# Router logits as four partial rows, tokens 0 to 127 last in a normalisation, and a token scatter issued in two pieces, in a two-layer hybrid decoder step

## What is computed

```python
x = layer_norm(ALPHA * x + mix, P['ln_mix_g'][l], P['ln_mix_b'][l])
...
logits = (jnp.einsum('btd,de->bte', x, router) + router_b).astype(jnp.float32)
probs = jax.nn.softmax(logits, axis=-1)
top_p, top_i = lax.top_k(probs, TOP_K)
...
for e in range(N_EXPERTS):
    y = y + gates[..., e:e + 1] * swiglu(x, w1[e], w3[e], w2[e]).astype(jnp.float32)
```

## Time and profile before

| what | value |
|---|---|
| three timed runs | 1055.07, 1058.78 and 1060.44 us, median 1058.78 us |
| the profiled execution | 1055.58 us, of it a span of 1053.8 us |
| granted TensorE clock, mean | 0.989 of full speed |
| PE busy | 1029.1 us, 98% of the span, 10347 records |
| DVE, ACT, POOL busy | 433.7, 182.0 and 94.2 us |
| memory traffic | 240.17 MB, mean 228 GB/s |

### The profile page before, as it was taken

The page is one execution under the profiler, slowest core; times in us unless marked ns, Lnnn a source line. Parts: engine busy times, 40 slices in busy tenths (PEclk is TensorE's granted clock), DMA queues, the critical chain, the costliest instruction groups (busy, mean ns, idle before and its releaser), DMA issues.

```text
span 1053.8 us, 22738 instructions
## 1 busy us (share of the span) xinstructions
PE 1029.1 (98%) x10347; PEld 736.3 (70%) x10347; DVE 433.7 (41%) x852; ACT 182.0 (17%) x393; POOL 94.2 (9%) x102
## 2 busy tenths in 40 slices
PE   9999999999999999999999999997999999999995
PEld 6787766999999999987877669743444444444452
DVE  5654635565656754256546352512011011010125
ACT  1322224031111100133322240500000000000011
POOL 2010123700000000000101200041000020000020
PEclk9999999999999999999999999898999999999998
DMA  9452239404443255013522348689999999999972
GB/s 340 139 200 81 80 104 328 188 2 165 169 183 155 81 192 223 2 45 116 201 81 80 104 140 356 250 333 325 419 403 412 405 400 405 424 421 392 413 281 81
DMA packets 36548, 240.17 MB, mean 228 GB/s; under 512 B 4768, under 2 KB 8096, under 8 KB 16736
## 3 DMA queue, kind: packets, MB, share of 16 engines
q1 hardware_dynamic: 26896, 216.40, 52.7%
q0 software_dynamic: 6416, 19.52, 5.3%
q10 hardware_dynamic: 3136, 2.75, 0.8%
HBM read 228.60 MB, written 13.07 MB: 229 GB/s over the span
## 4 chain that ended last, share of the span: by engine, by line
PE 90%; DVE 4%; DMA 3%; ACT 1%; issue 1%; POOL 1%; SPq 0%; DVEq 0%; POOLq 0%
PE ps L665 70%; PE ps L1165 14%; PE ps L1270 5%; PE ps L668 1%; DMA mix_or_moe<-expert_tokens 1%; DMA expert_tokens<-tables,slot_index 1%; DMA up_slots<-in_w_in 1%; DVE x L1979 1%; POOL expert_tokens L629 0%; DVE overlay L1974 0%; ACT overlay L1585 0%; DVE overlay L2110 0%; DVE up_slots L2081 0%; DVE mix_or_moe L2108 0%; POOL mix_or_moe L636 0%
## 5 line engine op out<-in xcount | busy, mean ns | idle before, releaser
L665 PE MATMUL ps<-up_slots,mix_or_moe 128*32 128x352 f32 (+2 forms) x3248 | 247.3, 453 | 5.6 <-DVE mix_or_moe L2672 5.6
L665 PE MATMUL ps<-x,up_slots 128*128 128x288 f32 (+2 forms) x944 | 233.3, 399 | 0.6 <-DMA up_slots<-in_w_in 0.6
L665 PEld LDWEIGHTS ps<-x,up_slots 128*128 128x128 f32 x944 | 169.0, 190 | 50.6 <-issue 8.3
L665 PEld LDWEIGHTS ps<-up_slots,mix_or_moe 128*32 128x32 f32 (+2 forms) x3248 | 100.8, 112 | 143.9 <-issue 136.0
L665 PE MATMUL ps<-overlay,tables 128*32 128x256 f32 (+4 forms) x2020 | 125.7, 375 | 0.3 <-ACT overlay L1585 0.3
L665 PEld LDWEIGHTS ps<-overlay,tables 128*32 128x32 f32 (+2 forms) x2020 | 72.9, 114 | 50.6 <-issue 5.5
L1165 PE MATMUL ps<-overlay,up_slots 128*128 128x144 f32 x704 | 91.2, 286 | 1.2 <-DVE overlay L2466 1.2
L1165 PEld LDWEIGHTS ps<-overlay,up_slots 128*128 128x128 f32 x704 | 88.3, 190 | 1.4 <-issue 1.4
L665 PE MATMUL ps<-overlay,up_slots 128*128 128x128 f32 (+3 forms) x560 | 86.0, 314 | 1.0 <-ACT overlay L1585 1.0
L665 PEld LDWEIGHTS ps<-overlay,up_slots 128*128 128x128 f32 x560 | 78.0, 191 | 8.6 <-ACT overlay L1585 1.9
L2690 DVE TENSOR_TENSOR mix_or_moe<-mix_or_moe,ps 128x352 f32<-128x352 f32 x24 | 11.2, 516 | 173.0 <-PE ps L665 173.0
(11 more groups left out here) (329 smaller groups left out, 902.0 us busy)
## 6 DMA issues: line engine op xcount, KB each, us to landing
up_slots<-in_moe_w SPq DMA_DIRECT2D x64, 1408.0 KB, 17.7
overlay<-in_moe_w SPq DMA_DIRECT2D x21, 1536.0 KB, 16.4
up_slots<-in_ffn_w SPq DMA_DIRECT2D x30, 1024.0 KB, 6.9
up_slots<-in_w_in SPq DMA_DIRECT2D x27, 1024.0 KB, 5.0
up_slots<-in_w_out SPq DMA_DIRECT2D x8, 1024.0 KB, 9.6
overlay<-in_moe_w SPq DMA_DIRECT2D x7, 1024.0 KB, 18.7
mix_or_moe<-in_states POOLq DMA_DIRECT2D x6, 512.0 KB, 10.1
out_sample_states<-mix_or_moe POOLq DMA_DIRECT2D x6, 512.0 KB, 6.0
```

The source lines that it names most:

```text
L665: return pe.matmul(o, lhsT, rhs, start=start, stop=stop)
```

## The change

It has two parts. In the router, the two token parts of this normalisation change places (160 columns first, tokens 0 to 127 last). The logits are made the other way round: a 128x32 block of router columns is the weights and the tokens move (160 or 128 columns), and feature tile k adds into the 32 partitions number k mod 4, so that four partial rows arise. DVE copies them out (`LGP`), and three products with a table (`groupsum`) add the four and turn tokens into rows. DVE then handles all three token tiles at once. Two single spins are added between the partial products, and the transposes of tokens 0 to 127 and of the sample tokens stand around the three products.

In the scatter, POOL waits for the first of the three transposes (`first_xe`) ahead of the first two transfers, and for the third (`xe_done`) ahead of the other four.

The diff, without the list of semaphore names:

```diff
@@ -47,7 +47,8 @@
 HALVES = slice(0, P), slice(P, T)
 TH = T // 2
 TOKEN_HALVES = slice(0, TH), slice(TH, T)
-LN_HALVES = TOKEN_HALVES, HALVES, HALVES
+LN_HALVES = TOKEN_HALVES, HALVES, HALVES[::-1]
+ROWS_ORDER = (1, 0, 2)
 NUP, KH, KD = 11, KT // 2, 11
 HALF_OUT, HALF_DOWN = 6, 5
 NCH = 4
@@ -315,6 +316,7 @@
         GTR = [MB[:, at:at + T] for at in (0, T, 8288)]
         YLAST = cut(MB, 2688, NG, CO)
 
+        LGP = MB[:, 8000:8000 + T]
         OH = cut(MB, 8000 + T, 3, CAP)
         hid_d = cut(MB, 3584, FT, T)
         sil_d = cut(TB, free_tb + NG * CO + 3 * D, 2, T)
@@ -622,8 +624,10 @@
             pool.wait_ge(S["xg_zeroed"], 16 * NE)
             pool.wait_ge(S["xtk_done"], 6)
             pool.wait_ge(S["idx_ready"], 1)
-            pool.wait_ge(S["xe_done"], 1)
+            pool.wait_ge(S["first_xe"], 1)
             for t in range(3):
+                if t == 1:
+                    pool.wait_ge(S["xe_done"], 1)
                 r = P if t < 2 else NS
                 for n in range(2):
                     pool.indirect_dma_start(XG, bass.IndirectOffsetOnAxis(ap=SLOT[0:r, n, t:t + 1], axis=0),
@@ -1333,9 +1337,9 @@
                         last = down_part(1, j, late, 0)
                     last.then_inc(S["down_ps"], 1)
 
-            def token_logits(t, k):
-                n = P if t < 2 else NS
-                return mm(PS[0:n, t, 0:NE], X[:, k, t * P:t * P + n], RW[:, k, 0:NE], k == 0, k == KT - 1)
+            def logit_parts(h, k):
+                j, c = k % NH, LN_HALVES[2][h]
+                return mm(PS[HR * j:HR * j + HR, h, 0:c.stop - c.start], RW[:, k], X[:, k, c], k < NH, k >= NH)
 
             def x_rows(t, i):
                 n = P if t < 2 else NS
@@ -1346,7 +1350,7 @@
             pe.wait_ge(S["columns_in"], 16)
             mean(2, 1, S["out_x"], 2 * HALF_OUT)
             spin(3, 4)
-            c = HALVES[1]
+            c = LN_HALVES[2][1]
             for k in range(KT):
                 if k % 4 == 0:
                     pe.wait_ge(S["ln_sq"], 4 * 2 + 2 + k // 4 + 1)
@@ -1354,21 +1358,29 @@
             last.then_inc(S["ln_var_ps"], 1)
             for k in range(KT):
                 x_half(2, 0, k)
-            x_rows(0, 0)
-            x_rows(0, 1)
+            x_rows(1, 0)
+            x_rows(1, 1)
             for k in range(KT):
-                last = token_logits(0, k)
+                last = logit_parts(0, k)
             last.then_inc(S["lgp_ps"], 1)
-            pe.wait_ge(S["xtk_done"], 2)
+            spin(1, 2)
             for k in range(KT):
                 x_half(2, 1, k)
-                token_logits(1, k)
-                last = token_logits(2, k)
+                last = logit_parts(1, k)
+                if k == 3:
+                    spin(1, 2)
             last.then_inc(S["lgp_ps"], 1)
-            for t in range(1, 3):
-                for i in range(2):
-                    x_rows(t, i)
-            spin(2, 3)
+            x_rows(0, 0)
+            pe.wait_ge(S["lgp_done"], 2)
+            for t in range(3):
+                n = P if t < 2 else NS
+                last = mm(PS[0:n, 0, t * NE:t * NE + NE], LGP[:, t * P:t * P + n], tb("groupsum"))
+            last.then_inc(S["logits_ps"], 1)
+            x_rows(0, 1)
+            for i in range(2):
+                x_rows(2, i)
+            pe.wait_ge(S["xtk_done"], 2)
+            spin(2, 4)
             pe.wait_ge(S["sel_done"], 1)
             sel = SEL.rearrange("p t e -> p (t e)")
             mm(PS[:, 0, 0:3 * NE], tb("before"), sel, True, False)
@@ -1378,7 +1390,7 @@
                 r = P if i < 2 else NS
                 last = mm(PS[0:1, 1, 0:NE], onesc[0:r, 0:1], SEL[0:r, i], i == 0, i == 2)
             last.then_inc(S["count_ps"], 1)
-            spin(1, 3)
+            spin(1, 4)
 
             def first_tokens():
                 pe.wait_ge(S["xtk_done"], 6)
@@ -1528,6 +1540,7 @@
                     n = P if t < 2 else NS
                     last = tr(PS[0:NE, 0, t * P:t * P + n], GTOK[0:n, t], n)
                 last.then_inc(S["d_gate_ps"], 1)
+                pe.sem_inc(S["first_xe"], 1)
                 pe.sem_inc(S["xe_done"], 1)
                 for e in range(1, NE):
                     pe.wait_ge(S[f"xgt_in_{e % 2}"], 64 * ((e + 1) // 2))
@@ -1758,7 +1771,7 @@
             def x_rows(t):
                 n = P if t < 2 else NS
                 for i in range(2):
-                    act.wait_ge(S["xtk_ps"], 2 * t + i + 1)
+                    act.wait_ge(S["xtk_ps"], 2 * ROWS_ORDER.index(t) + i + 1)
                     f(XTK[0:n, t, 512 * i:512 * i + 512], PS[0:n, 2 + 2 * t + i, :], ACT.Copy
                       ).then_inc(S["xtk_done"], 1)
 
@@ -1779,7 +1792,7 @@
                     shift_tiles(2, 1, 0, "ln_mix_b", range(6, KT))
                     deviation(2, 1)
                     act.wait_ge(S["states_stored"], 16 * STORES * DEPTH)
-                    x_rows(0)
+                    x_rows(1)
                     shift_tiles(2, 1, 1, "ln_mix_b", range(KT))
                 if l == 0:
                     def up_s5(n):
@@ -1819,7 +1832,7 @@
                     shifts(1, 0, 0, "ln_ffn_b")
                     squares(1, 1)
                     shifts(1, 0, 1, "ln_ffn_b")
-            x_rows(1)
+            x_rows(0)
             x_rows(2)
             act.wait_ge(S["lg_ready"], 1)
             f(E2, E2, ACT.Exp).then_inc(S["gate_exp"], 1)
@@ -2475,6 +2488,8 @@
                     scale_tiles(2, 1, 0, "ln_mix_g", range(6, KT))
                     v.memset(SM[:, 0:270], 0.0).then_inc(S["small_zeroed"], 1)
                     scale(2, 1, 1, "ln_mix_g")
+                    v.wait_ge(S["lgp_ps"], 1)
+                    cp(LGP[:, first], PS[:, 0, 0:first.stop - first.start]).then_inc(S["lgp_done"], 1)
                 if l == 0:
                     v.wait_ge(S["x_ready"], 2 * KT)
                     v.wait_ge(S["x_sums"], 1)
@@ -2587,21 +2602,15 @@
                     scale(1, 0, 1, "ln_ffn_g")
 
             v.wait_ge(S["small_zeroed"], 1)
-            def token_logits(t):
-                n = P if t < 2 else NS
-                return tt(LG[0:n, t], PS[0:n, t, 0:NE], RB[0:n, :], AD)
-
-            v.wait_ge(S["lgp_ps"], 1)
-            link(token_logits(0))
-            link(v.max(TOP[:, 0], LG[:, 0]))
-            v.max_index(TOPI[:, 0], TOP[:, 0], LG[:, 0])
             v.wait_ge(S["lgp_ps"], 2)
-            token_logits(1)
-            link(token_logits(2))
-            for t in range(1, 3):
+            cp(LGP[:, second], PS[:, 1, 0:second.stop - second.start]).then_inc(S["lgp_done"], 1)
+            v.wait_ge(S["logits_ps"], 1)
+            tt(LG[:, 0:2], PS[:, 0, 0:2 * NE].rearrange("p (t e) -> p t e", t=2), RB[:, :].unsqueeze(1).to_broadcast([P, 2, NE]), AD)
+            link(tt(LG[0:NS, 2], PS[0:NS, 0, 2 * NE:3 * NE], RB[0:NS, :], AD))
+            for t in range(3):
                 last = v.max(TOP[:, t], LG[:, t])
             link(last)
-            for t in range(1, 3):
+            for t in range(3):
                 last = v.max_index(TOPI[:, t], TOP[:, t], LG[:, t])
             link(last)
             iota = tb("iota8").unsqueeze(1).unsqueeze(1).to_broadcast([P, 2, 3, NE])
```

More of the change, by code:

```diff
@@ L85 @@
 x_sum ln_mean_ps ln_sq ln_fold ln_var_ps ln_xc ln_sd ln_xn z_xc dve_chain
-y_stored lgp_ps first_xe xtk_ps xtk_done flag_ready lg_ready xg_zeroed small_zeroed sel_done pos_ps count_ps places_done oh_ready oh_ps
+y_stored lgp_ps lgp_done logits_ps first_xe xtk_ps xtk_done flag_ready lg_ready xg_zeroed small_zeroed sel_done pos_ps count_ps places_done oh_ready oh_ps
 idx_ready gate_exp x_sent xgt_in_0 xgt_in_1 xe_done d_x d_x_ps u1_step u3_step u3_last ht_done dn_step
```

## The result

Before 1056.23 us (median of 7 runs, 1054.63 to 1060.44), after 1045.92 us (median of 7, 1044.64 to 1049.88): a ratio of 0.9902 with a 95% interval of 0.9882 to 0.9922. One run of the kernel before, of 3739.09 us, is left out of the ratios of this document. The forecast was 1047.0 us in a range of 1043.5 to 1055.0. The profiled execution of the changed kernel took 1044.64 us (a span of 1042.8, a mean clock of 0.995), 10.94 under the one before; the sum had said 10.3.

What follows compares the result with a forecast made beforehand. PE bounds nearly everywhere, losing time to a 5.6 us wait at expert 1 and half-clock stretches. Terms -2.9 - 5.6 - 1.84 = -10.3 gave 1045.3 off the profiled execution, 1048.5 off the median; forecast 1047 us, range 1043.5 to 1055.

Steps and rivals of the forecast that it cites:

- the sum: Whole kernel: -2.9 - 5.6 - 1.84 = -10.3 us, from the front, PE's wait at expert 1 and the low clock there.
- Swapped halves: Second mixing normalisation: 160 columns first puts the last residual about 2 us later, net +0.8, between 0 and +1.9.
- Logits: Router, last shift to DVE's start on the logits: about 1.45 us, 0.9 less than before, so DVE starts at 673.65.
- Up to the place products: PE's transposes and spins after the logits run at full clock: place products at 675.9 or 676.0, 2.9 us earlier.
- The front's term: Router up to expert 0's start: place products and expert 0 come 2.9 us earlier; about +0.7 if the clock stays low.
- Rival 1: Clock falls all the same, in the transposes before the place products; front about +0.4, total -7.0, 1048.6 us; chance 0.22.
- The scatter: POOL's first transfer 2.98 us earlier, last near 687.3, all six ahead of the refills at 688.5, landing in 3.9 to 5.
- The wait of 5.6 us and the 1.84: Expert 1: PE's wait for its tokens goes altogether (-5.6), and the low clock in its up products with it (-1.84).
- the 16.1 us of before: From the scatter's last landing to the end of expert 1's transposes: 16.1 us, kept unchanged; tokens ready at 708.1 or 713.7.
- rival 2: Expert 1's reads still held by the refills; half the wait and the low clock stay, -5.7, 1049.9 us; chance 0.15.
- Weights: Expert weight refills: 25.2 us each leaves about 13.8 of slack; PE draws 7.4 closer, so covered.
- rival 3: Weights become the bound: refills landing at 39 us make PE wait in experts 2 to 7, +8.1, 1063.7 us; chance 0.05.

Runs made afterwards that it cites:

- no_swap: The changed kernel with the old order of the halves in the second mixing normalisation, tokens 0 to 127 first; median 1046.74 us, ratio 0.9893.
- no_end_spins: The changed kernel without the two spins between the last transposes and the place products; median 1044.93 us, ratio 0.9910.
- refill_held: The kernel before, with SP holding the first weight refills until all six scatter transfers have landed; median 1052.28 us, ratio 0.9971.
- scatter_alone: The kernel before with only POOL's two scatter waits of the change, router and halves as before; median 1049.05 us, ratio 0.9914.
- scatter_second: The changed kernel with all six scatter transfers waiting for the second transpose; median 1048.19 us, ratio 0.9930.

## Why the prediction was right

*Swapped halves.* Mechanism right, size too large: the last residual came 1.61 later (662.79 against 661.18; I had about 2), and the last shift ended 0.35 later (671.71 against 671.36; I had 0.8). `no_swap` puts the price at expert 0 at 0.2.

*Logits.* DVE got them at 673.42; I had 673.65. The copy took 0.29 (0.3 forecast). From the last shift it took 1.71 where I had 1.45. That the sum still fits is luck: the shift's earlier end, 0.44, paid for the 0.26.

*Up to the place products.* I had 675.9, from PE's transposes and spins at full clock; it was 675.65. The front's term was -2.9 and came out -3.24. The clock rested on the 8-column products shrinking from 48 records to six, and that held; the spins, which I named with them as a reason, did nothing.

*Rival 1.* The rule set against the forecast, from the Trainium skill (TensorE: Matmul & The Clock Gate, Part 4: PE-mode transpose), isn't borne out by these traces: by that rule the clock should have fallen in or behind the stretch of transposes, and in `no_end_spins` it stayed at 1.00 with nothing else in it but six 8-column records, some 3.3 us in all. In `refill_held`, with the old router, it rose while PE ran transposes (its timeline, the clock over 679 to 682, and the first spins):

```profile
677.42 3.59 PE L669 MATMUL ps<-tables,x 128*128 128x128 f32 x16
679.00:682.00 3.00, 3.00 (x17) 2.29 (x15) 0.27 (x2) 2.29 (x5) 0.00 (x0) 0.70 1.02 427
680.85 1.14 PE L666 MATMUL ps<-tables 128*128 128x288 f32 x4
```

The clock is 0.50 from 677.4 to 680.5, and a mean of 0.70 over the 3 us is half clock for 1.8 of them, up to 680.8, so the full clock was there when the spins began. The prediction read from one trace that the full clock is there again only when two spins have followed the transposes; that doesn't hold in general. What a longer stretch of transposes does, no run shows.

*The scatter.* Right in each step: first transfer at 680.46, last at 686.82 (I had 687.3), no extra wait at the third (0.30 from issue to issue, as elsewhere), the refill at 688.17 (688.5), landing in 4.2 us (3.9 to 5). The wait of 5.6 and the 1.84 went, and `scatter_alone` and `refill_held` show that the refills were the cause. The Trainium skill (DMA: Bandwidth & Descriptors, Issuing engines are not separate DMA queues) says that transfers run on the same 16 DMA engines and interleave, whichever engine started them. The runs here agree and give it a price: medians of 3.9 to 4.4 us ahead of the refills, 8.5 and 8.6 around and behind the first ones.

*One step was mis-sized.* From the landing of the scatter to expert 1's tokens in place I kept the 16.1 us of before. It was 12.8 (from the last landing at about 690.0, 0.29 ahead of the reads, to 702.80, where the transposes that start at 701.10 end). The eight reads took 7.3 us at the median, where those of before took 11.2 (issues of 703 to 712):

```profile
mix_or_moe<-expert_tokens POOLq DMA_DIRECT2D x8, 96.0 KB, 11.2
```

They now set out between SP's second and third refill (689.36 and 695.27). Where refills set out beside them they were slow again, 12.1 in `scatter_second` (issues of 695.5 to 702) and 11.0 in `refill_held` (699 to 705); no run varies this alone. So the tokens are ready 7.6 us ahead of their use (expert 1 starts about 710.4), not 2.8, which is why rival 2 never came near.

*Weights.* I had refills of 25.2 us and 13.8 of slack, and counted 7.4 of it as drawn on. In the changed kernel the refills begun in 895 to 921 took 28.8, so 3.6 more, and PE shows no wait for them:

```profile
up_slots<-in_moe_w SPq DMA_DIRECT2D x5, 1408.0 KB, 28.8
```

In `refill_held` those of the same stretch took 34.2, still under the 39 at which I saw rival 3 decide. Its 1.9 us of waits came in the last expert, whose weights my term did not cover. So rival 3 was closer than I had it, and at a place where I hadn't looked.

The sum was -10.3 for the profiled execution; it came 10.94 lower. The difference lies in the front (0.33), in the overlap at the border of experts 0 and 1, where the products of expert 1 now start under the last of expert 0 (some 0.2: 57.01 for both against 28.61 + 28.57), and in 0.1 at the end. The forecast of 1047 stood between two starting points, because three runs left the median open; off the median of all seven, 1056.23, the same sum gives 1045.9. That this is the measured 1045.92 is closer than the terms were, and so is luck too.

## What to carry to other kernels

When PE waits for a small transfer, look at what else was issued around it: if a large prefetch sets out shortly after, moving the small one ahead of it by a few microseconds can be worth twice that (here 2.99 us gave 7.59), and moving both earlier together is worth nothing at that place. Look at the clock in stretches where PE is 100% busy: 24 products with 8 moving columns kept PE busy and were followed by half the clock, and making the small operand the weights took that away without any filler. Before adding fillers, leave them out once: here none of the four did anything that the trace shows.

## What was not expected

The clock also falls at other places, in some executions of a kernel and not in others. In the profile of `no_swap` it was low in a stretch of the mixer of layer 0 that its edit doesn't touch:

```profile
106.00:114.00 8.00, 8.00 (x38) 4.73 (x38) 4.53 (x9) 3.16 (x6) 0.00 (x0) 0.57 0.00 1
```

The changed kernel shows 1.00 in the same stretch, and its anchor comes at 635.89 where that of `no_swap` comes at 640.43. The mean clock of the timed executions goes the same way: 0.995 in that of 1044.64 us, 0.991 in that of 1049.88, both of the changed kernel. A single execution is thus uncertain by some microseconds, about the 5 us by which the runs of most kernels here differ, and a part of a microsecond can be compared only as a distance within a trace. What in the stretch ahead lets the clock fall, there or in the old logits, stays open: the runs show only after which work it fell.
